# One transformer block pair on one core: RWKV's and HGRN's preparation cut into more steps of the woven order, and narrower transfers for two weight chunks

## What is computed

```
q = silu(q_raw); f = lb + (1 - lb) * sigmoid(f_raw); k = 1 - f       # with one layer lb is 0
b = cumsum(log f) inside a chunk
o_inter = (q * exp(b)) @ state
scores[i, j] = sum_k q[i, k] * k[j, k] * exp(b[i, k] - b[j, k])   for j <= i
o = o_inter + scores @ i_raw; state = exp(b_last) * state + (k * exp(b_last - b))^T @ i_raw
```

```
cm = c + (c_prev - c) * mu                       # r, k, v and three low-rank inputs
w = -softplus(-(w0 + tanh(wd) @ w2)) - 0.5; decay = exp(-exp(w))
a = sigmoid(a0 + ad @ a2); g = sigmoid(gd) @ g2
kk = k * k_k / norm(k * k_k); k = k * (1 + (a - 1) * k_a)
state = state * decay + (state @ -kk) (kk * a)^T + v k^T; y = state @ r
```

## Time and profile before

| | us |
|---|---|
| median of 3 runs | 1541.99 (1540.57 to 1545.72) |
| the profiled execution | 1547.78, its span 1545.7 |
| PE busy | 1499.2 of the span, 97% |
| DVE, ACT, POOL busy | 1186.1, 869.7, 219.6 |
| mean granted clock of PE | 0.986 |
| bytes read from HBM | 258.83 MB |

### The profile page before, as it was taken

The page is one execution under the profiler, slowest core; times in us unless marked ns, Lnnn a source line. Parts: engine busy times, 40 slices in busy tenths (PEclk is TensorE's granted clock), DMA queues, the critical chain, the costliest instruction groups (busy, mean ns, idle before and its releaser), DMA issues.

```text
span 1545.7 us, 32239 instructions
## 1 busy us (share of the span) xinstructions
PE 1499.2 (97%) x10608; PEld 1332.3 (86%) x10608; DVE 1186.1 (77%) x2465; ACT 869.7 (56%) x1634; POOL 219.6 (14%) x167
## 2 busy tenths in 40 slices
PE   8799999999999899999999999999999999999997
PEld 8778887999877785798999999988888888888886
DVE  4788667889757577565499888889999777777777
ACT  5675545666558544665565566654444555555555
POOL 0001000011200001000078866620000000000000
PEclk9999999999999889999999999999999999999999
DMA  7434344565666610355567744467777666666665
GB/s 286 123 109 134 116 159 133 177 185 182 192 190 186 216 59 1 111 176 164 177 183 213 235 156 154 153 202 243 239 242 238 203 190 191 189 190 190 191 193 166
DMA packets 89292, 271.95 MB, mean 176 GB/s; under 512 B 9985, under 2 KB 27521, under 8 KB 88833
## 3 DMA queue, kind: packets, MB, share of 16 engines
q1 hardware_dynamic: 65520, 238.06, 49.3%
q10 hardware_dynamic: 23696, 32.87, 6.7%
HBM read 258.83 MB, written 12.06 MB: 175 GB/s over the span
## 4 chain that ended last, share of the span: by engine, by line
PE 89%; DVE 5%; ACT 3%; issue 1%; DMA 1%; ACTq 0%; DVEq 0%; SPq 0%
PE ps_chunk L508 17%; PE ps_misc L3049 12%; PE ps_chunk L501 10%; PE ps_misc L501 10%; PE ps_chunk L514 8%; PE ps_chunk L3166 7%; PE ps_misc L300 6%; PE ps_chunk L2000 4%; PE ps_chunk L3174 4%; PE ps_misc L2984 3%; PE ps_chunk L300 2%; PE ps_chunk L520 1%; DMA raw<-in_stream 1%; PE ps_misc L1027 1%; PE ps_chunk L529 1%
## 5 line engine op out<-in xcount | busy, mean ns | idle before, releaser
L425 ACT ACTIVATE w_hi<-raw 128x512 fp32r<-128x512 f32 (+2 forms) x654 | 399.9, 625 | 358.0 <-PE ps_chunk L514 143.4
L432 DVE TENSOR_TENSOR w_lo<-raw,w_hi 128x512 fp32r<-128x512 f32 (+2 forms) x516 | 352.5, 718 | 132.6 <-ACT w_hi L425 129.0
L508 PE MATMUL ps_chunk<-x_both,w_hi 128*128 128x256 f32 x2208 | 315.9, 285 | 0.5 <-ACT row L2875 0.5
L508 PEld LDWEIGHTS ps_chunk<-x_both,w_hi 128*128 128x128 f32 x2208 | 285.7, 192 | 0.9 <-issue 0.7
L432 POOL TENSOR_TENSOR w_lo<-raw,w_hi 128x512 fp32r<-128x512 f32 x140 | 182.2, 1314 | 257.6 <-DVE mixers_arena L2755 184.4
L514 PE MATMUL ps_chunk<-x_both,w_lo 128*128 128x256 f32 x1104 | 177.8, 283 | 0.0
L514 PEld LDWEIGHTS ps_chunk<-x_both,w_lo 128*128 128x128 f32 x1104 | 152.9, 193 | 0.0
L3264 DVE TENSOR_TENSOR w_lo<-raw,w_hi 128x512 fp32r<-128x512 f32 x120 | 83.0, 693 | 67.4 <-ACT w_hi L3218 67.3
L501 PE MATMUL ps_chunk<-w_hi,x_both 128*128 128x512 f32 (+1 forms) x392 | 124.0, 398 | 7.5 <-DVE w_lo L432 7.5
L3166 PE MATMUL ps_chunk<-x_both,w_hi 128*128 128x512 f32 x480 | 120.2, 392 | 0.0
L3218 ACT ACTIVATE w_hi<-raw 128x512 fp32r<-128x512 f32 x120 | 75.7, 631 | 63.5 <-PE ps_misc L501 63.3
(11 more groups left out here) (442 smaller groups left out, 2586.5 us busy)
## 6 DMA issues: line engine op xcount, KB each, us to landing
raw<-in_stream SPq DMA_DIRECT2D x452, 512.0 KB, 3.8
early_rows<-row ACTq DMA_DIRECT2D x68, 128.0 KB, 2.8
row<-early_rows ACTq DMA_DIRECT2D x66, 128.0 KB, 3.3
memory_kv<-mixers_arena ACTq DMA_DIRECT2D x4, 512.0 KB, 4.6
mixers_arena<-in_cmp_w ACTq DMA_DIRECT2D x1, 2048.0 KB, 11.0
mixers_arena<-memory_kv ACTq DMA_DIRECT2D x4, 512.0 KB, 6.3
row<-in_rows ACTq DMA_DIRECT2D x3, 512.0 KB, 5.4
mixers_arena<-in_consts ACTq DMA_DIRECT2D x1, 1441.0 KB, 8.1
```

Of the source, the lines that this page charges most:

```text
L425: e.activation(w_hi[q % 2][:, s], raw[q][:, s], ACT.Copy).then_inc(made, 1)
L432: e.tensor_tensor(w_lo[q % 2][:, s], raw[q][:, s], w_hi[q % 2][:, s].bitcast(F32), ALU.subtract).then_inc(made, 1)
L508: e.matmul(o, w[0][:, k * P:(k + 1) * P], x[:, k, :], start=k == 0 and x is x_hi, stop=False, skip_group_check=True)
```

## The change

Five things are changed.

- `feed` moves only the used columns of chunks 7 and 34: two runs of 1024 bytes per partition for chunk 7 and of 1120 bytes for chunk 34, in place of 4096 bytes. The loop over chunks is cut at the two, which are written out.
- RWKV: the shift and the mixes are split (tiles 6 and 7 first, the others in four later steps), tanh's table is asked for ahead, B-LW is computed right behind the scan (in PX, not X2), its exponentials and the three others come right behind the heads' sum, ahead of the root, the reciprocal is cut in two, and there are three more yields in all.
- HGRN: the five activations are spread over four steps, S is cleared by POOL, and the diagonal's products wait for the last activation alone, not for DVE. The predicated copy waits for the clearing.
- MIXERS_ORDER: its head is new, and has four r, five h and six d letters more than before. The rest is the old one, less six d letters near its end. There are 242 d letters before and after.
- Nothing else of the arithmetic is changed.

The diff:

```diff
--- before.py
+++ after.py
@@ -62,11 +62,11 @@
 BANK_BY_BANK = (0, 1, 4, 5, 2, 3, 6, 7)
 SUMS = ((0, 1, 16, 0), (1, 1, 8, 16), (2, 2, 8, 24), (4, 4, 4, 40), (8, 8, 1, 56))
 
-MIXERS_ORDER = ("ddddddddddddddddddddddddddmmddddddddddddrrrddddddrrrddmrddddmrdddddrddddddrrdddddddddhhdrdrhdrddhrrd"
-                "dhddhdrdhmdhdddddrhdhhdrhrrhddrddddhdrhhrdddhhdddrdhddhdddhrrdhdddhrhdddhhddhdhddrddrhddhhdrdddrhhdr"
-                "rrmmmhhrrmmrrrddddhdrdhrrhddrhhrddhhhhddhhhddhdrhddhhhrrhhhhrhhhrdhhdhdddddhhhhddhdddhhddddrdrddddhd"
-                "drhrdrdrdhdhrddddhrhrddddhddddrdrdddhrrrrhddrddhdrhrhhrhrdhddddddrddddhddddddddrddddddddrrdddddrdddd"
-                "ddddddddddddrhm")
+MIXERS_ORDER = ("ddddddddddddddddddddddddddmmddddddddddddrrrddddddrdrdrmrddrddddmrdrddrddrddrdddrddrdddddhhddhddhddrd"
+                "dhddrhdrdhrrddhddhdrdhmdhdddddrhdhhdrhrrhddrddddhdrhhrdddhhdddrdhddhdddhrrdhdddhrhdddhhddhdhddrddrhd"
+                "dhhdrdddrhhdrrrmmmhhrrmmrrrddddhdrdhrrhddrhhrddhhhhddhhhddhdrhddhhhrrhhhhrhhhrdhhdhdddddhhhhddhdddhh"
+                "ddddrdrddddhddrhrdrdrdhdhrddddhrhrddddhddddrdrdddhrrrrhddrddhdrhrhhrhrdhddddddrddddhddddddddrddddddd"
+                "drrdddddrddddddddddrhm")
 
 
 MEMORY_ORDER = ("dddnddddndddndndddddddaaddabbdddaabddabdddbaddbdaddaabeebbbedffeddddfddeddfddddddfedddfeeffddeeffddddddd"
@@ -381,17 +381,30 @@
 
 
         def feed(e):
-            def put(q, u):
+            def put(q, u, width=CW):
                 src = stream[u, :, :] if isinstance(u, int) else stream[bass.ds(u, 1), :, :].rearrange("a p n -> p (a n)")
-                e.dma_start(raw[q][:, :], src).then_inc(s_w[q], 16)
+                if width == CW:
+                    e.dma_start(raw[q][:, :], src).then_inc(s_w[q], 16)
+                else:
+                    used_of = lambda a: a.rearrange("p (half n) -> p half n", n=CW)[:, :, 0:width]
+                    e.dma_start(used_of(raw[q][:, :]), used_of(src)).then_inc(s_w[q], 16)
+
+            def chunk(n, width=CW):
+                for q in range(UNITS):
+                    e.wait_ge(s_lo1, n * UNITS + (q + 1 - UNITS))
+                    e.wait_ge(s_lo, n * UNITS + (q + 1 - UNITS))
+                    put(q, n * UNITS + q, width)
 
             for q in range(UNITS):
                 put(q, q)
-            with e.Fori(1, chunk_at[0]) as i:
-                for q in range(UNITS):
-                    e.wait_ge(s_lo1, i * UNITS + (q + 1 - UNITS))
-                    e.wait_ge(s_lo, i * UNITS + (q + 1 - UNITS))
-                    put(q, i * UNITS + q)
+            at = 1
+            for narrow in sorted(widths):
+                with e.Fori(at, narrow) as i:
+                    chunk(i)
+                chunk(narrow, widths[narrow])
+                at = narrow + 1
+            with e.Fori(at, chunk_at[0]) as i:
+                chunk(i)
 
         sp.steps.append(feed)
 
@@ -1352,22 +1365,24 @@
             state = picks[:, 0:2, :].rearrange("p a (h n) -> p (a h) n", n=P)
 
             yield from evacuated(4, act, dve)
+            pool.do(lambda e: e.memset(S, 0.0))
             cleared = pool.do(lambda e: e.memset(KL, 0.0))
             act.do(lambda e: e.activation(LF, zf, ACT.Abs))
             act.do(lambda e: e.activation(LF, LF, ACT.Exp, scale=-1.0))
+            yield
             a = act.do(lambda e: e.activation(LF, LF, ACT.Ln, bias=c("one")))
+            yield
             act.do(lambda e: e.activation(K, zf, ACT.Sigmoid, scale=-1.0))
-            act.do(lambda e: e.activation(zq, zq, ACT.Silu))
+            yield
+            with_k = act.do(lambda e: e.activation(zq, zq, ACT.Silu))
             yield
             dve.do(lambda e: e.scalar_tensor_tensor(out=LF, in0=zf, scalar=0.0, in1=LF, op0=ALU.min,
                                                     op1=ALU.subtract), a)
             dve.do(lambda e: e.tensor_tensor_scan(B, restart, LF, 0.0, ALU.mult, ALU.add))
-            dve.do(lambda e: e.memset(S, 0.0))
-
 
             for level in range(-1, LEVELS):
                 if level < 0:
-                    q_l, k_l, mask, v = zq, K, by_block[:, LEVELS, :], dve.now()
+                    q_l, k_l, mask, v = zq, K, by_block[:, LEVELS, :], None
                 else:
                     b = 2 << level
                     view = lambda a, b=b: a.rearrange("p (m b) -> p m b", b=b)
@@ -1390,12 +1405,12 @@
                 for i in range(8):
                     for chunk in chunks:
                         of_both = slice(i * P + chunk.start, i * P + chunk.stop)
-                        done = pe.do(mm(ps[chunk, i * HG_C:(i + 1) * HG_C], k_l[:, of_both], q_l[:, of_both]), v, act.now(),
-                                     *free)
+                        done = pe.do(mm(ps[chunk, i * HG_C:(i + 1) * HG_C], k_l[:, of_both], q_l[:, of_both]),
+                                     *([v, act.now()] if v else [with_k]), *free)
                 yield
                 v = dve.do(lambda e, ps=ps, mask=mask: e.copy_predicated(
                     S, mask.bitcast(U32).unsqueeze(1).broadcast_to([P, 8, HG_C]),
-                    ps.rearrange("p (a b) -> p a b", b=HG_C)), done)
+                    ps.rearrange("p (a b) -> p a b", b=HG_C)), done, cleared)
                 banks.release(at, 1, v)
 
             yield
@@ -1533,13 +1548,21 @@
             yield from evacuated(2, act, dve)
             for lane in (pe, dve, pool):
                 lane.wait(loaded[12])
-            dve.do(lambda e: e.tensor_tensor(shift[:, :, 1:T], zc[:, :, 0:T - 1], zc[:, :, 1:T], ALU.subtract))
-            dve.do(lambda e: e.tensor_scalar(shift[:, :, 0:1], zc[:, :, 0:1], -1.0, None, ALU.mult))
-            for k in (6, 7, 0, 1, 2, 3, 4, 5):
-                if k == 0:
-                    low_rank = dve.now()
-                dve.do(lambda e, k=k: e.scalar_tensor_tensor(out=CM[:, k, :], in0=shift[:, k, :], scalar=c("rwkv_mu", k),
-                                                             in1=zc[:, k, :], op0=ALU.mult, op1=ALU.add))
+            act.quiet(lambda e: e.activation(ss[:, 15:16], c("one"), ACT.Tanh))
+
+            def shifted(some):
+                dve.do(lambda e: e.tensor_tensor(shift[:, some, 1:T], zc[:, some, 0:T - 1], zc[:, some, 1:T], ALU.subtract))
+                dve.do(lambda e: e.tensor_scalar(shift[:, some, 0:1], zc[:, some, 0:1], -1.0, None, ALU.mult))
+
+            def mixed_in(*tiles):
+                for k in tiles:
+                    dve.do(lambda e, k=k: e.scalar_tensor_tensor(out=CM[:, k, :], in0=shift[:, k, :],
+                                                                 scalar=c("rwkv_mu", k), in1=zc[:, k, :], op0=ALU.mult,
+                                                                 op1=ALU.add))
+
+            shifted(slice(6, 8))
+            mixed_in(6, 7)
+            low_rank = dve.now()
             rr, kk, vv = (CM[:, 2 * n:2 * n + 2, :] for n in range(3))
             rr, kk = flat(rr), flat(kk)
 
@@ -1547,6 +1570,7 @@
             act.do(lambda e: e.activation(th[0:64, :], CM[0:64, 6, :], ACT.Tanh), low_rank)
             yield
             a = act.do(lambda e: e.activation(sg, CM[:, 7, :], ACT.Sigmoid))
+            shifted(slice(0, 6))
             wa, g2 = lora[:, 0:256], lora[:, 256:512]
             yield
             at, ps, free = banks.take(2)
@@ -1557,6 +1581,7 @@
             for j in range(2):
                 act.do(lambda e, j=j, ps=ps: e.activation(LW[:, j * T:(j + 1) * T], ps[:, j * T:(j + 1) * T], ACT.Sigmoid,
                                                    bias=c("rwkv_w0", j)), done)
+                mixed_in(2 - 2 * j, 3 - 2 * j)
                 yield
                 a = act.do(lambda e, j=j, ps=ps: e.activation(A[:, j * T:(j + 1) * T], ps[:, 512 + j * T:512 + (j + 1) * T],
                                                        ACT.Sigmoid, bias=c("rwkv_a0", j)))
@@ -1565,8 +1590,10 @@
             for t in range(TT):
                 gdone = pe.do(mm(gps[:, t * T:(t + 1) * T], sg[:, t * P:(t + 1) * P], g2), *free)
             g_tok = act.do(lambda e: e.activation(flat(G), gps, ACT.Copy), gdone)
+            mixed_in(4, 5)
             banks.release(gate_at, 1, g_tok)
 
+            yield
             dve.do(lambda e: e.tensor_scalar(LW, LW, -RK_DECAY_SCALE, None, ALU.mult), a)
             dve.do(lambda e: e.tensor_tensor_scan(B, restart[:, 0:512], LW, 0.0, ALU.mult, ALU.add))
             tiles = B.rearrange("p (m b) -> p m b", b=RK_C)
@@ -1578,6 +1605,7 @@
                                              decay[:, :, RK_C + RK_C // 2 - 1:RK_C + RK_C // 2], ALU.add))
             dve.do(lambda e: e.tensor_tensor(tiles[:, :, in_front], tiles[:, :, in_front],
                                              middle.broadcast_to([P, 4, RK_C // 2]), ALU.subtract))
+            centred = dve.do(lambda e: e.tensor_tensor(PX, B, LW, ALU.subtract))
 
             for j in range(2):
                 s = slice(j * T, (j + 1) * T)
@@ -1587,11 +1615,18 @@
             yield
```

(17 more changed lines are left out.)

## The result

| | before | after |
|---|---|---|
| median of 4 runs | 1541.28 (1540.57 to 1545.72) | 1579.45 (1579.02 to 1581.7) |
| ratio to before, 95% interval | | 1.0252 [1.0227, 1.0278] |
| profiled execution, its span | 1547.78, 1545.7 | 1579.76, 1577.6 |
| mean granted clock | 0.986 | 0.978 |

A forecast was written before the change was run, and what follows sets the result against it. PE was taken as busy nearly throughout, with about 11 us to win before 90 us and little spare DVE time after. Terms 4.4 + 1.6 + 1.5 - 0.5 gave +7.0 us, so 1549.0, range 1535 to 1556.

The forecast's parts named there:

- There the order matches the old one again: After the six cut dense letters are made up at the order's end, strands were claimed back at their old places.
- The six dense letters: End of token chunks: HGRN's last level and RWKV's inversion lose six dense steps (4.4 us) as cover; plus 1.5 us.
- +4.4 for longer gaps: Edited stretch before 100 us: PE idle time rises from 9.57 to 14.0 us.
- RWKV's preparation: RWKV up to its transposes: first gap (2.65 us) goes, DVE bounds, PE then waits 3.3, 0.2 and 6.3 us.
- The gap at 47: PE's 2.65 us wait for the sigmoid before RWKV's low-rank products, claimed to go: minus 2.65 us.
- rival A: Faster: finer cuts work, AB product within 2 us of PE's arrival, no clock lost; 1535.3 us, chance 0.22.
- HGRN's activations: Before HGRN's first products: an added Exp table load, only Silu moving behind unit 19's split; PE gap 4.2 us.
- The clock: Lower granted clock after the three longer PE gaps: 3.2 us against 1.6, plus 1.6 us (bounds -1.6 and +6).
- The transfers: Narrow chunks 7 and 34: nothing for 7; near 500 us only a tail competes, minus 0.5 us (0 to -7.5).
- Rival D: Tail of chunk 34's narrow transfers held the late unit, so gap and slow clock go: -7.5, 1542.0 us, chance 0.07.
- Rival C: The forecast itself, all terms as summed: 1549.0 us, alone from 1546.6 to 1556, chance 0.43.
- The six idle letters: Dense letters 130 to 135 do nothing, since the memory tokens come only with m10 at letter d135.

## Why the prediction was wrong

**The step that failed** is "There the order matches the old one again", in the part on the end of the token chunks. The letters match, the work behind them doesn't: RWKV is a step early. I had compared places in the string and not the number of yields before them. The surplus r, which had no term and no rival, measured 25.8 us in the change and 34 on the old code.

**The six dense letters** had the term +1.5, with bounds 0 and 4.4. With the r aligned, moving them back measured 5.6, a little above the upper bound. That is a net figure, since in front the letters give cover.

**The size of the rest** was near. Without the surplus letter the change costs 10.6 us (1553.69 against 1543.07), and I had 7.0. The terms were not as near, so this is in part luck: of +4.4 for longer gaps +0.6 came, and the six letters cost 5.6 for 1.5.

**RWKV's preparation.** The gap at 47 went as forecast (2.65 to 0.38). I had 3.3, 0.2 and 6.3 for the three waits up to the transposes, 9.8 in all. Measured are 2.72 and 5.40, 8.1. That DVE bounds this part and that spreading only moves the wait was right, and rival A (1535.3) falls with it: its condition was an AB product within 2 us of PE, and PE waited 5.40.

**HGRN's activations.** I had 4.2 and it was 1.66. I had taken the strand's first letter for a step with work, but it only runs up to the first yield. So Ln, Sigmoid and Silu stand at dense steps 71, 73 and 77, the scan at 79 and the products at 81. Sigmoid, too, stands behind unit 19's split, as the timeline of ACT shows.

```profile
79.96 1.05 ACT L1370 ACTIVATE mixers_arena<-mixers_arena 128x1024 f32<-128x1024 f32 x1
81.02 1.28 ACT L1371 ACT_TABLE_LOAD   x1
82.32 1.06 ACT L1371 ACTIVATE mixers_arena<-mixers_arena 128x1024 f32<-128x1024 f32 x1
83.40 1.28 ACT L1373 ACT_TABLE_LOAD   x1
84.69 1.15 ACT L1373 ACTIVATE mixers_arena<-mixers_arena,col 128x1024 f32<-128x1024 f32 x1
...
86.22 1.14 ACT L438 ACTIVATE w_hi<-raw 128x512 fp32r<-128x512 f32 x2
87.38 1.28 ACT L1375 ACT_TABLE_LOAD   x1
```

Sigmoid and its load are 2.34 (1.28 and 1.06), and 4.2 less 2.34 is 1.86, close to the measured 1.66. The load ahead of Exp that I had forecast is there at 81.02. The following start is 1.30 us after a load's, as before, and the load itself starts as the activation ahead of it ends (79.96 and 1.05, then 81.02). The Trainium skill's drain of about 1.38 us beside each load (ScalarE: Activation LUTs, What ACT_TABLE_LOAD costs) doesn't show here either.

**The clock.** I had +1.6 for this stretch. It fell behind the gaps, as windows of the changed kernel show:

```profile
56.00:60.00 4.00, 3.31 (x10) 2.28 (x11) 3.10 (x6) 3.88 (x7) 0.00 (x0) 0.57 0.23 37
...
68.00:76.00 8.00, 2.70 (x13) 2.71 (x14) 6.07 (x10) 1.19 (x2) 0.00 (x0) 0.63 0.23 68
...
86.00:90.00 4.00, 2.34 (x12) 2.31 (x11) 1.29 (x2) 3.97 (x6) 0.00 (x0) 0.64 0.05 14
```

What it cost is seen in the products behind the gaps. Before, they ran at the full clock:

```profile
58.41 1.02 PE L300 MATMUL ps_misc<-mixers_arena 128*128 128x512 f32 x2
...
79.42 1.53 PE L1027 MATMUL ps_misc<-ident_iota,mixers_arena 128*128 128x128 f32 x12
```

In the change the same products take 2.08 and 2.82: 2.4 us more. Otherwise the clock was low mostly while PE was idle, where it costs nothing: in the 8 us at 0.63 PE was busy for only 2.70. Up to dense step 81 I had +6.0 (4.4 and 1.6), and with the 48 matmuls that moved behind it about 2.6 was measured. The difference is in the gaps, +0.6 for +4.4.

**The transfers.** I took -0.5 between 0 and -7.5, and nothing was measured. In the change the gap is 1.83, and its delay falls there from 35.5 us (chunk 34's first products) to 33.0 (the next chunk's); as the gap is 1.06 in a kernel with the old transfers, this can't be put down to them. Rival D falls by the time of the transfers alone.

Rival C had the right sign, but for a cause that it didn't hold. The six idle letters were as I had said.

## What to carry to other kernels

Where an order is written out by hand, a new yield shifts everything behind it. Count yields against letters for each strand, and compare not the letters but which step of each strand runs at which place; one shifted step cost 1.5 to 3.3% here, more than twice the 11 us or so that the edit could win at most. Before cutting a block finer, see whether the engine that runs it is the bound of its stage: if so, the wait only moves. And when a changed kernel loses time in code that wasn't edited, look first at what stands ahead of the late instruction in its engine's queue.

## What was unexpected, and what stays open

Small idle gaps in many places can cost more than their sum. In the change between 96 and 290 us 21 us of added idle time came with a fall of the granted clock from 0.99 to 0.93. With the r aligned, 5.6 us of added idle time (188.67 less 183.11) came with none (1.00). Windows of the changed kernel around three of its gaps:

```profile
150.00:156.00 6.00, 4.50 (x64) 4.01 (x66) 3.81 (x10) 2.02 (x5) 0.00 (x0) 0.72 0.01 4
...
190.00:200.00 10.00, 8.31 (x45) 7.80 (x46) 4.99 (x13) 1.19 (x3) 0.00 (x0) 0.66 0.09 35
...
244.00:254.00 10.00, 5.62 (x22) 4.86 (x21) 5.47 (x7) 2.23 (x4) 0.00 (x0) 0.68 0.01 2
```

The clock is the third number from the end; before, it was 1.00 from 134 to 151 us.

Open is which of RWKV's displaced steps costs most, since only the whole strand was shifted. So is whether the narrow transfers do anything to the gap near 500 us, which differs from kernel to kernel without them. Nor is it settled why the kernels with the old places and the new code gain nothing that can be measured, though gaps shrink: their single runs spread by some 10 us (1535.44 to 1545.85 for the first of them), more than the gaps are worth. Even the kernel before and the one with the transfers alone, which up to there differ only in chunk 7's transfers, are 1.1 us apart to dense step 193 in their traces (209.1 and 208.0). None clearly beats the kernel before; the nearest, at 0.9983, has an interval that ends at 0.9999.
